# Stick-breaking attention: the sum over later tiles in high and low parts, on TensorE

## The chip, the cores and the metric

One NeuronCore of a Trainium2 chip runs the whole program. The metric is the device time of one execution in microseconds (us); of several executions the median is given. The engines are called by the profile's names: PE is TensorE (PEld its weight loads), DVE is VectorE, ACT is ScalarE, POOL is GpSimd, SP is SyncE.

## What is computed

The program is a stack of layers over 512 tokens of width 1024 in float32: a Mamba layer, a sparse-attention layer, their feed-forward parts, and then a second block with three mixers side by side. The change touches one of these mixers, stick-breaking attention with 8 heads of width 64:

```
z = einsum("bqhd,bkhd->bhqk", q[:, q0:k_len], k[:, :k_len]) * scale
mask = s_idx[None, :] < t_idx[:, None]
log_1m = where(mask, log_sigmoid(-z), 0.0)
after = cumsum(log_1m, axis=3, reverse=True) - log_1m
att = where(mask, exp(log_sigmoid(z) + after), 0.0)
out = einsum("bhqk,bkhd->bqhd", att, v[:, :k_len])
```

With softplus(z) = -log_sigmoid(-z), the exponent is z minus the sum of softplus(z) over the key itself and all later keys before the query. That sum over keys is what the changed lines compute.

## The kernel before, in words

Every engine has its own instruction stream, written out by hand; semaphores join them. The dense products (`product`, L282) take weights and inputs as a high part and a low part in the type fp32r, and make three products of them (high by high, high by low, low by high), each of 512 columns.

The stage of the change is `sb_tensor` (L2047), `sb_scalar` (L2119) and `sb_vector` (L2162). Keys lie on the 128 partitions, queries along the columns. Since only earlier keys count, key tile 0 meets 512 queries, tile 1 meets 384, tile 2 meets 256 and tile 3 meets 128: 1280 columns a head, spread over three PSUM banks (`ZT`, `IN_BANK`, `ZB`; two sets of banks, used by heads in turn).

For head n the steps are:

- PE: the scores z, four f32 products of 64 rows (L2080), and a bf16 product of identity and mask for each diagonal tile (L2085).
- ACT: the absolute value of each bank into `s_e` (L2143), then over all 1280 columns at once the exponential of minus that (L2146) and the logarithm of one plus that (L2148).
- DVE: the softplus, max(z, 0) + `s_e`, bank by bank into `s_sp` (L2180), two buffers in turn. Then three sums of 128 columns of tiles further on (L2186, L2187, L2189) into `sq`, as `later_sums` lays out, so that PE need not add tile by tile.
- PE: subtracts the sums in the same banks. `ntri`, a triangle of minus ones, takes each tile's own part (L2096: four f32 products, of 512, 384, 128 and 256 columns). `nones`, all minus ones, takes the later tiles (L2100: five f32 products over 768 columns in all).
- ACT: the exponential of each bank into `s_e` (L2153).
- PE: the products with the values, for two heads together (L2115, `values_of_pair`); ACT (L2160) and DVE (L2172) split the result in a high and a low part.

On PE the order is: scores of head n, sums of head n-1, the values of a pair when n is odd and at least 3, scores of head n+1. The scores of head n+1 write the banks that head n-1 used, so each bank waits for its exponential at L2153. On ACT the order is: absolute values, exponential and logarithm of head n, and then the exponentials of head n-1. The next stage's products wait for the last `yb_lo` (L2200). The scores of head 7 are followed on PE by the sums of head 6, the values of heads 4 and 5, the sums of head 7, and the values of heads 6 and 7.

Of the kernel before, what the change touches and what calls it, by code (L numbers as in the profile page):

```python
# [6 lines left out]
ALU = mybir.AluOpType  # L7
ACT = mybir.ActivationFunctionType
AX = mybir.AxisListType
F32 = mybir.dt.float32  # L10
# [3 lines left out]
P = 128  # L14
T = 512
# [125 lines left out]
def build(nc, dram):  # L141
    units, at = unit_list()
    NU = len(units)
    with ExitStack() as ctx:
# [3 lines left out]
        def sbuf(name, width, dt=F32, scope=ctx, parts=P):  # L148
            return scope.enter_context(nc.sbuf_tensor(name, [parts, width], dt))
# [1405 lines left out]
        g_row, g_row2, g_cum = g_qs[0], g_qs[1], g_qs[3]  # L1555
        blk = ctx.enter_context(ExitStack())
        s_q, s_k = sbuf("s_q", 4 * T, scope=blk), sbuf("s_k", 4 * T, scope=blk)
        s_sp = [sbuf(f"s_sp{i}", 1280, scope=blk) for i in range(2)]
        s_e = [sbuf("s_e0", 1280, scope=blk)]
        s_identb, s_negb = sbuf("s_identb", P, BF16, scope=blk), sbuf("s_negb", P, BF16, scope=blk)  # L1560
        blk.close()
        blk = ctx.enter_context(ExitStack())
        sbuf("below_yc", 16 * KC * T // 4, scope=blk)
        s_e += [sbuf(f"s_e{i}", 1280, scope=blk) for i in (1, 2, 3)]
        blk.close()
        s_vt = mod_w

# [461 lines left out]

        ZT = [(0, 0, 0, 512), (1, 0, 512, 384), (2, 0, 1024, 256), (1, 384, 896, 128)]  # L2030
        uS = at["sb"]
        later_done = S("later_done")

        def later_sums(m):

            return sq[:, m % 2 * T:m % 2 * T + 2 * P], sq[:, m % 2 * T + 2 * P:m % 2 * T + 3 * P]

        def later_keys(m):

            sp, (of0, of1) = s_sp[m % 2], later_sums(m)  # L2040
            o1, o2, o3 = (ZT[i][2] for i in (1, 2, 3))
            return (((0, 1, sp[:, o1:o1 + P]), (0, 2, of0)), ((1, 1, sp[:, o2:o2 + P]), (1, 2, of1)),
                    ((2, 1, sp[:, o3:o3 + P]),))

        IN_BANK = ((0,), (1, 3), (2,))

        def sb_tensor(pe):  # L2047
            def aux(t):
                pe.wait_ge(bx_done, t + 1)
                if t == 8:  # L2050
                    pe.wait_ge(go_done, 4)
                if t >= 10:
                    pe.wait_ge(bt_done, t - 9)
                for s in range(TT):
                    ins = pe.transpose((B4, B5)[t % 2][:, s * P:(s + 1) * P], sq[:, (t % 2) * T + s * P:(t % 2) * T + (s + 1) * P], ident)
                ins.then_inc(b_aux, 1)

            for t in range(1, 12):
                if t >= 2:
                    pe.wait_ge(bx_done, t - 1)  # L2060
                product(pe, uS + t, h_hi, h_lo)
                if t <= 4:
                    stat_sums(pe, *norms[f"gdn_{t - 1}"], 1)
                if t >= 9:
                    aux(t - 1)
            aux(11)
            pe.wait_ge(bx_done, 12)
            pe.wait_ge(bt_done, 4)
            pe.wait_ge(gnrm, 4)
            pe.wait_ge(smask_done, 2)  # L2070
            for n in range(10):
                if n < 8:
                    t, hs = n // 2, slice(n % 2 * 64, n % 2 * 64 + 64)
                    for b, tiles in enumerate(IN_BANK):
                        if n >= 2:
                            pe.wait_ge(ea_done, 3 * (n - 2) + b + 1)
                        out = ZB[n % 2][b]
                        for i in tiles:
                            _, c, o, w = ZT[i]
                            pe.matmul(out[:, c:c + w], s_k[hs, t * T + i * P:t * T + (i + 1) * P],  # L2080
                                      s_q[hs, t * T + i * P:(t + 1) * T], start=(i != 3), stop=False,
                                      skip_group_check=True)
                        for i in tiles:
                            c = ZT[i][1]
                            ins = pe.matmul(out[:, c:c + P], s_identb[:, :], s_negb[:, :], start=False, stop=False,  # L2085
                                            skip_group_check=True)
                        ins.then_inc(z_mm, 1)
                if 1 <= n < 9:
                    m = n - 1
                    pe.wait_ge(sp_done, m + 1)  # L2090
                    pe.wait_ge(later_done, 3 * m + 3)
                    for b, tiles in enumerate(IN_BANK):
                        out, keys = ZB[m % 2][b], later_keys(m)[b]
                        for i in tiles:
                            _, c, o, w = ZT[i]
                            pe.matmul(out[:, c:c + w], cst("ntri"), s_sp[m % 2][:, o:o + w], start=False,  # L2096
                                      stop=(i == 3), skip_group_check=True)
                        for i, j, src in keys:
                            c = ZT[i][1]
                            ins = pe.matmul(out[:, c + j * P:c + j * P + src.shape[1]], cst("nones"), src, start=False,  # L2100
                                            stop=(i == 2 or j == 2), skip_group_check=True)
                        ins.then_inc(acc_mm, 1)
                if n >= 3 and n % 2:
                    values_of_pair(pe, (n - 3) // 2)
# [57 lines left out]
        def sb_vector(v, link):  # L2162
            v.tensor_copy(s_identb[:, :], ident).then_inc(smask_done, 1)
            v.tensor_scalar(s_negb[:, :], cst("strict"), 1.0, -NEG, ALU.subtract, ALU.mult).then_inc(smask_done, 1)
            for t in range(8, 12):
                v.wait_ge(b_aux, t - 7)
                v.tensor_copy(s_vt[:, :].rearrange("p (s c) -> p s c", s=TT)[:, :, (t - 8) * P:(t - 7) * P],
                              (B4, B5)[t % 2][:, :].rearrange("p (s c) -> p s c", s=TT)).then_inc(bt_done, 1)
# [5 lines left out]

            for n in range(8):
                v.wait_ge(ln_done, n + 1)
                if n >= 2:
                    v.wait_ge(acc_mm, 3 * n - 3)
                for b, (o, w) in enumerate(ZPARTS):
                    ins = v.scalar_tensor_tensor(s_sp[n % 2][:, o:o + w], ZB[n % 2][b][:, 0:w], 0.0,  # L2180
                                                 s_e[n % 4][:, o:o + w], ALU.max, ALU.add)
                ins.then_inc(sp_done, 1)
                sp, (of0, of1) = s_sp[n % 2], later_sums(n)
                o1, o2, o3 = (ZT[i][2] for i in (1, 2, 3))
                v.wait_ge(sp_done, n + 1)
                v.tensor_tensor(of1, sp[:, o2 + P:o2 + 2 * P], sp[:, o3:o3 + P], ALU.add).then_inc(later_done, 1)  # L2186
                v.tensor_tensor(of0[:, 0:P], sp[:, o1 + P:o1 + 2 * P], sp[:, o2:o2 + P], ALU.add).then_inc(later_done, 1)  # L2187
                v.wait_ge(later_done, 3 * n + 2)
                v.tensor_tensor(of0[:, P:2 * P], sp[:, o1 + 2 * P:o1 + 3 * P], of1, ALU.add).then_inc(later_done, 1)  # L2189
                if n >= 4 and n % 2 == 0:  # L2190
                    low((n - 4) // 2)
            low(2)
# [820 lines left out]
```

## Time and profile before

| what | value |
|---|---|
| three runs | 2622.99, 2623.27, 2633.18 us; median 2623.27 |
| the profiled execution | 2631.3 us |
| its span | 2629.5 us |
| PE, DVE, ACT, POOL busy | 97%, 46%, 41%, 37% of the span |

### The profile page before, as it was taken

How to read it: one execution, taken by the hardware profiler on the slowest of the kernel's cores; microseconds unless marked ns; L12 is line 12 of the kernel's file. 1: busy time of each engine (PE TensorE's matmuls, PEld its weight loads, DVE VectorE, ACT ScalarE, POOL GpSimd, SP SyncE). 2: the span in 40 equal slices, each digit the busy share in tenths (PEclk: the TensorE clock that was granted, in tenths of full speed). 3: DMA queues.
4: the chain of work that ended last, by engine and by line, in shares of the span. 5: the costliest groups of instructions: out<-in, count | busy, mean ns of one | idle time of the engine just before them, and what ended most of it. 6: DMA issues, size and time to landing. Idle time of an engine off the chain costs nothing.

```text
span 2629.5 us, 37049 instructions
## 1 busy us (share of the span) xinstructions
PE 2538.4 (97%) x13464; PEld 2065.5 (79%) x13464; DVE 1208.7 (46%) x2023; ACT 1069.2 (41%) x1679; POOL 961.2 (37%) x427
## 2 busy tenths in 40 slices
PE   7999989999999989999999999999999999999998
PEld 5777768877888756669888888788668888988887
DVE  4877776577555746655111127654222112631112
ACT  3366644322225346654222226733442323542232
POOL 0333334455464310013444353302214455353453
PEclk9999999999999999999999999999999999999999
DMA  6533334577653310011333231201113333132331
GB/s 249 181 112 115 104 125 138 175 233 231 217 191 111 120 35 28 19 34 57 111 97 100 92 112 57 81 17 41 57 33 100 106 107 112 64 111 86 99 105 56
DMA packets 76195, 277.35 MB, mean 105 GB/s; under 512 B 8576, under 2 KB 11264, under 8 KB 74528
## 3 DMA queue, kind: packets, MB, share of 16 engines
q1 hardware_dynamic: 57104, 202.71, 23.7%
q10 hardware_dynamic: 18960, 72.82, 8.0%
q8 instruction: 91, 1.49, 0.2%
q14 instruction: 40, 0.33, 0.0%
HBM read 272.55 MB, written 2.16 MB: 104 GB/s over the span
## 4 chain that ended last, share of the span: by engine, by line
PE 79%; DVE 9%; issue 4%; DMA 4%; ACT 3%; ACTq 1%; DVEq 0%
PE G L295 28%; PE STAT_G L295 26%; DMA mod_w<-in_modw 2%; DVE mod_w L334 2%; PE B L308 2%; PE B L295 2%; PE B L602 2%; PE B L2423 1%; PE B L1357 1%; PE STAT_G L308 1%; PE NRM L1394 1%; PE G L308 1%; ACTq L1123 1%; PE G L602 1%; PE STAT_G L1375 1%
## 5 line engine op out<-in xcount | busy, mean ns | idle before, releaser
L280 POOL TENSOR_TENSOR w_lo<-raw,w_hi 128x1024 fp32r<-128x1024 f32 x371 | 922.4, 2497 | 1617.2 <-ACT w_hi L272 1550.9
L272 ACT ACTIVATE w_hi<-raw 128x1024 fp32r<-128x1024 f32 x375 | 386.3, 1051 | 304.0 <-PE STAT_G L295 132.2
L295 PE MATMUL G<-h_hi,w_hi 128*128 128x512 f32 x872 | 346.1, 397 | 0.9 <-DVE tn L1001 0.9
L295 PE MATMUL STAT_G<-h_hi,w_hi 128*128 128x512 f32 x856 | 338.0, 395 | 4.4 <-ACT mod_w L1242 1.5
L295 PE MATMUL G<-h_lo,w_hi 128*128 128x512 f32 x872 | 340.2, 390 | 0.0
L295 PE MATMUL G<-h_hi,w_lo 128*128 128x512 f32 x872 | 340.1, 390 | 0.0
L295 PE MATMUL STAT_G<-h_hi,w_lo 128*128 128x512 f32 x856 | 333.4, 389 | 0.0
L295 PE MATMUL STAT_G<-h_lo,w_hi 128*128 128x512 f32 x856 | 333.1, 389 | 0.0
L334 DVE SCALAR_TENSOR_TENSOR mod_w<-mod_w,const 128x1024 f32<-128x1024 f32 x96 | 189.2, 1990 | 50.0 <-DMA mod_w<-in_modw 49.8
L295 PEld LDWEIGHTS G<-h_hi,w_hi 128*128 128x128 f32 x872 | 164.3, 188 | 40.3 <-issue 7.3
L295 PEld LDWEIGHTS STAT_G<-h_hi,w_hi 128*128 128x128 f32 x856 | 160.7, 188 | 40.2 <-issue 4.7
L295 PEld LDWEIGHTS G<-h_lo,w_hi 128*128 128x128 f32 x872 | 164.3, 188 | 34.3 <-issue 1.4
L295 PEld LDWEIGHTS G<-h_hi,w_lo 128*128 128x128 f32 x872 | 164.0, 188 | 34.5
L295 PEld LDWEIGHTS STAT_G<-h_hi,w_lo 128*128 128x128 f32 x856 | 160.8, 188 | 33.8
L295 PEld LDWEIGHTS STAT_G<-h_lo,w_hi 128*128 128x128 f32 x856 | 160.8, 188 | 33.6 <-issue 1.2
L941 ACT ACTIVATE u_hi<-tn 128x512 f32 (+1 forms) x76 | 48.0, 632 | 256.4 <-DVE tn L1001 220.5
L295 PE MATMUL G<-u_hi,w_hi 128*128 128x512 f32 x376 | 147.0, 391 | 0.3 <-issue 0.3
L295 PE MATMUL G<-u_hi,w_lo 128*128 128x512 f32 x376 | 146.3, 389 | 0.0
L295 PE MATMUL G<-u_lo,w_hi 128*128 128x512 f32 x376 | 146.3, 389 | 0.0
L295 PE MATMUL STAT_G<-u_hi,w_hi 128*128 128x512 f32 (+1 forms) x320 | 125.8, 393 | 3.6 <-ACT y L2574 2.7
L295 PE MATMUL STAT_G<-u_lo,w_hi 128*128 128x512 f32 (+1 forms) x320 | 125.1, 391 | 0.0
L295 PE MATMUL STAT_G<-u_hi,w_lo 128*128 128x512 f32 (+1 forms) x320 | 125.0, 391 | 0.0
(581 smaller groups left out, 4440.4 us busy)
## 6 DMA issues: line engine op xcount, KB each, us to landing
raw<-in_units SPq DMA_DIRECT2D x373, 512.0 KB, 3.6
mod_w<-in_modw ACTq DMA_DIRECT2D x96, 512.0 KB, 4.7
acsb<-acs ACTq DMA_DIRECT2D x16, 512.0 KB, 3.7
mod_first<-in_modw ACTq DMA_DIRECT2D x6, 1024.0 KB, 22.5
cw<-in_cw ACTq DMA_DIRECT2D x2, 2048.0 KB, 9.0
x<-in_x SPq DMA_DIRECT2D x2, 1024.0 KB, 12.3
mod_first<-in_modw SPq DMA_DIRECT2D x2, 1024.0 KB, 25.0
raw<-in_units ACTq DMA_DIRECT2D x2, 512.0 KB, 18.8
```

Of the source, the lines that this page charges most:

```text
L272: act.activation(w_hi[s][:, :], raw[s][:, :], ACT.Identity).then_inc(hi_done, 1)
L280: pool.tensor_tensor(w_lo[s][:, :], raw[s][:, :], w_hi[s][:, :].bitcast(F32), ALU.subtract).then_inc(lo_done, 1)
L295: ins = pe.matmul(out[0:m, :], a[s][:, k * P:k * P + m], b[:, c], start=(n == 0 and q == 0), stop=(n == len(blocks) - 1 and q == 2))
L308: ins = pe.matmul(out[:, tokens[a]], w[s][:, k * P:(k + 1) * P], b[:, at_tokens(k, a)], start=(k == 0 and q == 0), stop=(k == n - 1 and q ...
L334: ins = v.scalar_tensor_tensor(half_row, half_row, 1.0, silc, ALU.mult, ALU.mult, accum_out=mod[:, bass.ds(g * 2 + b, 1)] if not isinstanc ...
L602: ins = pe.matmul(banks[e][0:m[e], tokens[a]], w[s][:, k * P:k * P + m[e]], b[:, at_tokens(k, a)], start=(k == 0 and q == 0), stop=(k == K ...
L941: act.activation(u_hi[g % 2][:, bass.ds(i * (body * T) + j * T, T)], tn[:, (k % 2) * T:(k % 2 + 1) * T], ACT.Identity).then_inc(hh_done, 1)
L1123: act.dma_start(swapped[t % 2][h + a:h + a + 8, :], src[h + b:h + b + 8, :]).then_inc(turn_in[t % 2], 16)
L1357: pe.matmul(out[:, h * T:h * T + w], qr[t % 2][hs, qt * P:w], keys[hs, j * T:j * T + w], start=True, stop=False, skip_group_check=True)
L1375: ins = pe.transpose(TB_[:, o], pr[b % 3][:, o], ident)
L1394: ins = pe.matmul(OB_[hs, qt * P:(qt + 1) * P], vals[:, s * 256 + hd * 64:s * 256 + (hd + 1) * 64], ptr[b % 2][:, h * T + s * P:h * T + (s ...
L2423: ins = pe.matmul(Y[j][64 * hh:64 * hh + 64, s * P:T], xdt[j][:, s * P + 64 * hh:s * P + 64 * hh + 64], seg[:, hh * 1280 + o:hh * 1280 + o ...
```

## The change

`s_sp` and the partial sums in `sq` go. The softplus is written in place over `s_e`. DVE then writes a high part `s_hi` (a copy of all 1280 columns to fp32r) and a low part `s_lo` (`s_e` minus `s_hi`, 1280 columns), one buffer of each. PE multiplies both parts by an fp32r copy of the two constants (`s_minus`, made once by DVE). With no partial sums, PE takes every later tile by itself: the all-ones products are now of 384, 256 and 128 columns for tile 0, 256 and 128 for tile 1, and 128 for tile 2.

```diff
-        s_sp = [sbuf(f"s_sp{i}", 1280, scope=blk) for i in range(2)]
+        s_hi, s_lo = sbuf("s_hi", 1280, F32R, scope=blk), sbuf("s_lo", 1280, F32R, scope=blk)
...
+        s_minus = sbuf("s_minus", 2 * P, F32R, scope=blk)
...
+        LATER_KEYS = (((0, 1, 1), (0, 2, 2), (0, 3, 3)), ((1, 1, 2), (1, 2, 3)), ((2, 1, 3),))
+        KEY_TILE = {1: (512, 384), 2: (1024, 256), 3: (896, 128)}
...
                     pe.wait_ge(sp_done, m + 1)
-                    pe.wait_ge(later_done, 3 * m + 3)
                     for b, tiles in enumerate(IN_BANK):
-                        out, keys = ZB[m % 2][b], later_keys(m)[b]
+                        out = ZB[m % 2][b]
                         for i in tiles:
                             _, c, o, w = ZT[i]
-                            pe.matmul(out[:, c:c + w], cst("ntri"), s_sp[m % 2][:, o:o + w], start=False,
-                                      stop=(i == 3), skip_group_check=True)
-                        for i, j, src in keys:
-                            c = ZT[i][1]
-                            ins = pe.matmul(out[:, c + j * P:c + j * P + src.shape[1]], cst("nones"), src, start=False,
-                                            stop=(i == 2 or j == 2), skip_group_check=True)
+                            for part in (s_hi, s_lo):
+                                pe.matmul(out[:, c:c + w], s_minus[:, 0:P], part[:, o:o + w], start=False,
+                                          stop=(i == 3 and part is s_lo), skip_group_check=True)
+                        for i, j, key in LATER_KEYS[b]:
+                            c, (o, w) = ZT[i][1], KEY_TILE[key]
+                            for part in (s_hi, s_lo):
+                                ins = pe.matmul(out[:, c + j * P:c + j * P + w], s_minus[:, P:2 * P], part[:, o:o + w],
+                                                start=False, stop=(key == 3 and part is s_lo), skip_group_check=True)
                         ins.then_inc(acc_mm, 1)
...
             v.tensor_scalar(s_negb[:, :], cst("strict"), 1.0, -NEG, ALU.subtract, ALU.mult).then_inc(smask_done, 1)
+            a = CONST["ntri"]
+            v.tensor_copy(s_minus[:, :], const[:, a:a + 2 * P]).then_inc(smask_done, 1)
...
                 v.wait_ge(ln_done, n + 1)
-                if n >= 2:
-                    v.wait_ge(acc_mm, 3 * n - 3)
+                e = s_e[n % 4]
                 for b, (o, w) in enumerate(ZPARTS):
-                    ins = v.scalar_tensor_tensor(s_sp[n % 2][:, o:o + w], ZB[n % 2][b][:, 0:w], 0.0,
-                                                 s_e[n % 4][:, o:o + w], ALU.max, ALU.add)
-                ins.then_inc(sp_done, 1)
-                sp, (of0, of1) = s_sp[n % 2], later_sums(n)
-                o1, o2, o3 = (ZT[i][2] for i in (1, 2, 3))
-                v.wait_ge(sp_done, n + 1)
-                v.tensor_tensor(of1, sp[:, o2 + P:o2 + 2 * P], sp[:, o3:o3 + P], ALU.add).then_inc(later_done, 1)
-                v.tensor_tensor(of0[:, 0:P], sp[:, o1 + P:o1 + 2 * P], sp[:, o2:o2 + P], ALU.add).then_inc(later_done, 1)
-                v.wait_ge(later_done, 3 * n + 2)
-                v.tensor_tensor(of0[:, P:2 * P], sp[:, o1 + 2 * P:o1 + 3 * P], of1, ALU.add).then_inc(later_done, 1)
+                    ins = v.scalar_tensor_tensor(e[:, o:o + w], ZB[n % 2][b][:, 0:w], 0.0, e[:, o:o + w],
+                                                 ALU.max, ALU.add)
+                link(ins)
+                if n:
+                    v.wait_ge(acc_mm, 3 * n)
+                v.tensor_copy(s_hi[:, :], e[:, :]).then_inc(sp_hi, 1)
+                v.wait_ge(sp_hi, n + 1)
+                v.tensor_tensor(s_lo[:, :], e[:, :], s_hi[:, :].bitcast(F32), ALU.subtract).then_inc(sp_done, 1)
```

`link` marks an instruction and lets DVE wait until it has ended. `acc_mm` counts the banks whose sums are subtracted, three a head.

## Rows read from the trace of the kernel before

**Rows 1.** The page: an engine's busy share, and the chain's shares by engine.

```profile
PE 2538.4 (97%) x13464; PEld 2065.5 (79%) x13464; DVE 1208.7 (46%) x2023; ACT 1069.2 (41%) x1679; POOL 961.2 (37%) x427
PE 79%; DVE 9%; issue 4%; DMA 4%; ACT 3%; ACTq 1%; DVEq 0%
```

**Rows 2.** Windows: length, each engine's busy time (instructions), granted clock, DMA share, GB/s.

```profile
1876.00:1947.00 71.00, 68.86 (x304) 39.82 (x304) 21.94 (x53) 46.05 (x69) 0.00 (x0) 0.93 0.00 1
...
335.00:340.00 5.00, 4.28 (x17) 1.81 (x18) 3.69 (x6) 3.04 (x4) 3.65 (x2) 0.66 0.03 7
1885.00:1890.00 5.00, 5.00 (x15) 2.94 (x16) 1.49 (x6) 3.96 (x5) 0.00 (x0) 0.62 0.02 3
1890.00:1907.00 17.00, 16.97 (x85) 10.34 (x83) 6.55 (x18) 11.72 (x18) 0.00 (x0) 1.00 0.00 0
```

**Rows 3.** The chain of work through the stage: start, duration, engine, tile, line.

```profile
1886.28 1.81 PE B L2096 x2
...
1891.13 1.05 PE B L2080 x2
...
1893.40 0.22 PE B L2085 x2
...
1894.41 0.91 PE B L2096 x2
...
1897.97 1.12 PE B L2080 x2
...
1901.33 0.91 PE B L2096 x2
...
1904.64 0.22 PE B L2100 x2
1904.86 2.31 PE G L2115 x16
1907.17 1.05 PE B L2080 x2
...
1933.40 0.91 PE B L2096 x2
...
1939.24 1.05 PE B L2096 x2
...
1942.95 0.39 ACT s_e L2153
```

**Rows 4.** The timeline, ACT and DVE in the loop.

```profile
1883.41 1.62 DVE L2180 SCALAR_TENSOR_TENSOR s_sp<-B,s_e 128x512 f32<-128x512 f32 x3 [7.17 <-ACT s_e L2148]
...
1897.34 0.58 ACT L2153 ACTIVATE s_e<-B 128x512 f32<-128x512 f32 x1
...
1904.38 0.69 DVE L2180 SCALAR_TENSOR_TENSOR s_sp<-B,s_e 128x512 f32<-128x512 f32 x1 [4.44 <-ACT s_e L2148]
...
1906.04 0.29 DVE L2186 TENSOR_TENSOR sq<-s_sp 128x128 f32<-128x128 f32 x1
```

**Rows 5.** The chain elsewhere: fp32r products, 256 columns (L602) and 512 (L295).

```profile
452.06 0.71 PE B L602 x6
...
1952.92 5.44 PE G L295 x24
```

**Rows 6.** Groups of DVE by shape: busy, mean ns of one, idle before.

```profile
L2664 DVE TENSOR_SCALAR seg<-acsb,atok 128x512 f32<-128x512 f32 x32 | 15.4, 481 | 0.0
L2664 DVE TENSOR_SCALAR seg<-acsb,atok 128x128 f32<-128x128 f32 x32 | 9.0, 281 | 0.0
L2676 DVE TENSOR_TENSOR seg<-seg,cbm 128x1280 f32<-128x1280 f32 x32 | 46.2, 1487 | 1.4 <-ACT seg L2545 1.4
```

**Rows 7.** The timeline of DVE ahead of the loop.

```profile
1842.52 0.22 DVE L2164 TENSOR_SCALAR s_negb<-const 128x128 bf16<-128x128 f32 x1
1862.81 0.69 DVE L2167 COPY mod_w<-B 128x512 f32<-128x512 f32 x1 [20.06 <-PE B L2055]
```

More of the change, by code:

```diff
@@ L2031, in build @@
         uS = at["sb"]
[L2032 to L2040, printed above, removed]
-            o1, o2, o3 = (ZT[i][2] for i in (1, 2, 3))
-            return (((0, 1, sp[:, o1:o1 + P]), (0, 2, of0)), ((1, 1, sp[:, o2:o2 + P]), (1, 2, of1)),
-                    ((2, 1, sp[:, o3:o3 + P]),))
+        sp_hi = S("sp_hi")
+        LATER_KEYS = (((0, 1, 1), (0, 2, 2), (0, 3, 3)), ((1, 1, 2), (1, 2, 3)), ((2, 1, 3),))
+        KEY_TILE = {1: (512, 384), 2: (1024, 256), 3: (896, 128)}
         IN_BANK = ((0,), (1, 3), (2,))
@@ L2069, in sb_tensor @@
             pe.wait_ge(gnrm, 4)
-            pe.wait_ge(smask_done, 2)
+            pe.wait_ge(smask_done, 3)
             for n in range(10):
@@ L2176, in sb_vector @@
                 v.wait_ge(ln_done, n + 1)
-                if n >= 2:
-                    v.wait_ge(acc_mm, 3 * n - 3)
+                e = s_e[n % 4]
                 for b, (o, w) in enumerate(ZPARTS):
-                    ins = v.scalar_tensor_tensor(s_sp[n % 2][:, o:o + w], ZB[n % 2][b][:, 0:w], 0.0,
-                                                 s_e[n % 4][:, o:o + w], ALU.max, ALU.add)
-                ins.then_inc(sp_done, 1)
-                sp, (of0, of1) = s_sp[n % 2], later_sums(n)
-                o1, o2, o3 = (ZT[i][2] for i in (1, 2, 3))
-                v.wait_ge(sp_done, n + 1)
-                v.tensor_tensor(of1, sp[:, o2 + P:o2 + 2 * P], sp[:, o3:o3 + P], ALU.add).then_inc(later_done, 1)
-                v.tensor_tensor(of0[:, 0:P], sp[:, o1 + P:o1 + 2 * P], sp[:, o2:o2 + P], ALU.add).then_inc(later_done, 1)
-                v.wait_ge(later_done, 3 * n + 2)
-                v.tensor_tensor(of0[:, P:2 * P], sp[:, o1 + 2 * P:o1 + 3 * P], of1, ALU.add).then_inc(later_done, 1)
+                    ins = v.scalar_tensor_tensor(e[:, o:o + w], ZB[n % 2][b][:, 0:w], 0.0, e[:, o:o + w],
[6 more added lines that the diff above has]
+                v.tensor_tensor(s_lo[:, :], e[:, :], s_hi[:, :].bitcast(F32), ALU.subtract).then_inc(sp_done, 1)
                 if n >= 4 and n % 2 == 0:
```

## The prediction

> **What bounds the kernel now.** I read the page first, then the windows, then the chain and the timeline of the stage. PE is busy for 97% of the span and carries 79% of the chain [rows 1], so time saved on PE counts, unless another engine ends last in the stage at hand. The stage with the changed lines lies between 1876 and 1947 us: 71 of 2629.5 us, with POOL idle and a mean granted clock of 0.93 [rows 2]. Whatever the change does must happen in those 71 us, 2.7% of the span. A difference of 0.5%, 13 us, is about what a measurement of this kernel can tell from no change; it would take 18% of the stage.
>
> In the chain the stage looks like PE alone [rows 3]. The timeline shows a second engine close behind. There are two kinds of steps. In a short step PE goes from the scores of head n to the sums of head n-1 and then to the scores of head n+1. The sums of head 1 start at 1894.41 and the scores of head 3 at 1897.97, 3.56 us later [rows 3]. Meanwhile ACT makes absolute value, exponential and logarithm of head 2, and only then, at 1897.34, the first exponential of head 1, which ends at 1897.92 [rows 4] and frees the bank that the scores of head 3 write. **ACT and PE end within 0.05 us of each other.** In a long step, the values of a pair stand between: sums at 1901.33, values at 1904.86, scores at 1907.17 [rows 3], 5.84 us, and there ACT is done long before. The scores take 3.36 us after a short gap (1897.97 to 1901.33), and 3.28 us after a long one, as the loop's period shows: the four sums between heads 1 and 7 that start a pair lie (1933.40 - 1901.33)/2 = 16.04 us apart [rows 3], and 16.04 = 3.56 + 3.36 + 5.84 + 3.28.
>
> **The sums on PE.** Now they take 1904.86 - 1901.33 = 3.53 us a head [rows 3]. The new ones are 20 fp32r products, two each of ten shapes: one of 512 columns, two of 384, three of 256, four of 128. At the higher clock, 2.4 GHz, 24 products of 512 take 5.44 us, 0.227 each, and six of 256 take 0.71, 0.119 each [rows 5]. Between them I take 0.173 for 384. No fp32r product of 128 columns is shown. 
>
> **The work on DVE.** Softplus stays as it is: three instructions, whose start lies 3.05 us after the end of the scores (1904.38 against 1901.33) and whose successor starts 1.66 us later, at 1906.04 [rows 3, 4], that is 4.71 us after the scores. Three small sums go. A copy of 1280 columns comes; the SBUF-only single-source rows give 481 ns for 512 columns and 281 for 128 [rows 6], 0.52 ns a column and 0.21 us fixed: 0.88 us for 1280. If the fp32r output or some other thing keeps it from that pace, it costs like a two-source instruction, 1.49 us. Below, nothing better than 0.88 is shown; I take no gain. The subtraction has two sources and 1280 columns: 1.49 us [rows 6]. With 0.04 us at each handover the low part is ready for PE at 4.71 + 0.88 + 0.04 + 1.49 + 0.04 = 7.16 us after the end of the scores.
>
> The Trainium skill has a rule for the copy (VectorE: DVE Perf Modes, What auto-detection actually checks): a single source with source and destination in SBUF runs at two elements a cycle, a two-source f32 operation at one. The rows' slopes agree, 0.52 ns a column on the one and about 1.2 per column all told on the other [rows 6]; whether fp32r as output is within the rule, no row shows.
>
> **The new wait.** The copy waits for the sums of the head before (`acc_mm`), since there is one buffer. Queued behind it on DVE are the copy, the subtraction and at times the split of a pair's result; PE's next sums wait for them. In a short step these sums end 2.74 us after the scores, before the softplus is done at 4.71, so the wait costs nothing. If that cover went, it would cost what the sums overran. The constant's copy is one DVE instruction ahead of the loop, like the 0.22 us ones there, and 20.06 us of idle time follow [rows 7]: nothing, and uncovered some 0.3 us. DMAs, SP and POOL are not touched; ACT's work is the same.
>
> **Put together.** A short step stays at 3.56 us: PE is done 0.8 us sooner, but ACT's exponential, 3.5 us after the scores, holds the next scores. After these scores, 3.56 + 3.36 = 6.92 us after the last ones, PE wants the low part and gets it at 7.16: a new wait of 0.24 us. The long step then costs 2.74 + 2.31 + 3.28. A pair takes 7.16 + 8.33 = 15.49 us against 16.04, **0.55 less**. There are two such pairs up to the scores of head 6: 1.10 us.
>
> At the start: softplus of head 0 starts at 1883.41 [rows 4] and ends at 1885.07; the low part is ready at 1885.07 + 2.45 = 1887.52, where the sums started at 1886.28 [rows 3]. The clock is at its lower level, 1.2 GHz, until about 1888.8 (granted 0.62 between 1885 and 1890, 1.00 after) [rows 2]. So 1.28 us yield 0.64 of the 2.74, the rest takes 2.10: the next scores start at 1890.90 against 1891.13, a gain of 0.23.
>
> At the end the values of heads 4 and 5 follow the sums of head 6, and then come the sums of head 7, with no scores between as cover. They start 5.84 us after the scores now (1939.24 against 1933.40) [rows 3] and 7.16 after: 1.32 lost, which eats the 0.23 + 1.10 gained. What is left is the last sums: now 1939.24 to the end of the last exponential at 1943.34 [rows 3], 4.10 us. After, the first bank's sums take 1.26 us, the exponentials of two banks follow at 0.60 each or as the sums allow, and the last, of 0.39, ends at 3.30. Gain 0.80. **Sum: 0.23 + 1.10 - 1.32 + 0.80 = 0.8 us faster.** Against the profiled execution's own 2631.3 that is 2630.5; it is 8 us above the median of the runs, with the stage the same, and against the median 2623.27 it is **2622.5**.
>
> **Rivals.**
>
> - **The low part comes later or narrow products are dear.** A copy of 1.49 us costs 0.61 more at four places (the start, the waits for heads 2 and 4, head 7): 2.4 us, giving 2624.9. Narrow products at 0.22 add 0.88 in three places and 0.7 at the end, 3.3 us: 2625.8. Both: 2628.2. For it: no row shows either operation with fp32r.
> - **The narrow products are cheap**, 0.07: 0.32 less at three places and some 0.3 at the end, 2621.2. If, against the timeline, ACT did not hold the short steps, all eight sums would save 0.8 to 1.1 us each, and the time would be 2614 to 2617. Against it: the 0.05 us between ACT's exponential and the scores.
> - **TensorE's clock falls in the loop: slower.** At the start of the loop PE ran at 1.2 GHz for some 10 us after a gap. The change puts new idle gaps into PE's stream: 1.2 us at the start, 1.1 us in each pair, 1.3 at the end. If the clock stayed low for the loop, PE's 14.4 us a pair (3.36 + 3.28 + 2 x 2.74 + 2.31) would become 28.9 and a pair lose 12.8 against now; over three pairs and a half, some 45 us: 2668. It passes 13 us where about 26 us of the stage's full-clock work run at the lower clock. Against it: PE stays 93% busy in the new loop, and low clock appears in short stretches (0.66 over 5 us, with 4.28 busy, is 3.4 us at half) [rows 2], worth 1.7 us each; one or two of these are possible, 2624 to 2626. The Trainium skill (TensorE: Matmul & The Clock Gate, HAM oscillation) says that idle gaps between bursts of products bring the clock to half; it speaks against this change, and its oscillation in every step would be the 2668.
> - **The change does not do what it says**: the products run at f32's pace after all, 5120 columns at twice two records' price, about 8.5 us a head. That is 5 us more in each of eight: 2663. The dense products of the same type at 0.227 [rows 5] speak against it.
>
> **How the numbers follow.** Chances: the forecast with its small terms either way (2621 to 2624) 0.60; dear copy or dear narrow products 0.18; cheap narrow products or free short steps 0.08; a short loss of clock 0.09; clock low through the loop 0.03; f32's pace 0.01; a gain of over 13 us out of this stage, for which I see no term, 0.01. Clock and f32's pace are slower by over 0.5%: 0.04. Faster by over 0.5%: 0.01. The rest is within 0.5%: 0.95. The range starts at 2619.5, under the cheap products by some 1.5 for what an unshown price hides. Upward, both dear terms give 2628 and a stretch of low clock 2630; and one of the three runs of before lies 9.9 above the median, as the profiled one lies 8.0 above, so a median of after may fall there: 2633.
>
> **What would show it.** Right: sums (L2096 and L2100's successors) of 2.7 us a head; the copy at 0.88 and the subtraction at 1.49; in short steps the scores still waiting for ACT's exponential; a wait of DVE's low part of 0.2 us in each pair, and of 1.3 at head 7; pairs 15.5 us apart; one stretch of low clock at the start. Wrong: pairs 16 us or more apart, low clock after 1890, sums over 3.5 us, or short steps of under 3.5 us.

## The result and the profile after

The changed kernel takes 2629.48 us, median of 20 runs (2624.69 to 2637.75), against 2624.56 us for the kernel before (20 runs, 2621.57 to 2633.18). The ratio is 1.0019, with a 95% interval of 1.0011 to 1.0027: **4.9 us slower**, where 0.8 us faster was forecast. The profiled execution took 2634.37 us, its span is 2632.6 us. In the two traces the difference lies in the stage of the change: its loop starts 1.0 us earlier after the change (1875.36 against 1876.35), the next stage starts 3.1 us later, and from there to the end both take 682.3 us. Up to 1850 us the granted clock is 0.99 in both, with PE busy for 1773.95 us before and 1774.36 after. The work ahead of the loop differs by more than the change from one execution to the next: in the 14 profiled executions of this study the loop starts between 1864.6 and 1876.5 us. So a single time says little here; medians, and distances inside the stage, say more.

On the page of the changed kernel PE's busy time is unchanged and DVE's is 13 us longer; the lines answer to [rows 1].

```profile
PE 2537.8 (96%) x13480; PEld 2071.7 (79%) x13480; DVE 1221.4 (46%) x2016; ACT 1069.2 (41%) x1679; POOL 961.6 (37%) x427
PE 79%; DVE 9%; issue 4%; ACT 3%; DMA 3%; ACTq 1%; DVEq 0%
```

Shorter sums should have lowered PE's busy time. That they did not is the first hint: the new products took longer than their price. The windows of the stage show why (columns: length, PE busy and instructions, granted clock, DMA share, GB/s). First the changed kernel, then the kernel before, whose rows list all engines' busy times ahead of the clock:

```profile
1875.00:1892.00 17.00, 15.44 (x45) 0.60 0.00 1
1892.00:1900.00 8.00, 7.22 (x36) 1.00 0.00 1
1900.00:1905.00 5.00, 4.97 (x19) 0.66 0.00 0
1905.00:1917.00 12.00, 11.22 (x64) 1.00 0.00 1
1917.00:1922.00 5.00, 4.88 (x19) 0.66 0.00 0
1922.00:1934.00 12.00, 11.21 (x64) 1.00 0.00 0
1934.00:1939.00 5.00, 4.86 (x19) 0.66 0.01 3
1939.00:1950.00 11.00, 9.01 (x64) 1.00 0.00 0
```

```profile
1875.00:1892.00 17.00, 16.17 (x48) 8.25 (x47) 5.84 (x14) 9.60 (x13) 0.00 (x0) 0.70 0.02 7
1892.00:1909.00 17.00, 16.97 (x80) 10.03 (x80) 4.81 (x12) 11.26 (x17) 0.00 (x0) 1.00 0.00 1
1909.00:1926.00 17.00, 16.97 (x83) 10.05 (x81) 5.41 (x13) 11.57 (x19) 0.00 (x0) 1.00 0.00 0
1926.00:1943.00 17.00, 16.89 (x85) 10.71 (x83) 5.41 (x13) 11.60 (x19) 0.00 (x0) 1.00 0.00 1
```

Before, the clock is at its lower level, 1.2 GHz, only at the loop's start, for 10.2 us ((1 - 0.70)/0.5 x 17). After, it stays there for 13.7 us at the start and falls again **behind each of the three short steps**, for 3.4 us each time ((1 - 0.66)/0.5 x 5). The chain shows what lies under these stretches (start, duration, engine, tile, line; L2073 is the scores, L2089 and L2094 the sums, L2109 the values):

```profile
1891.63 1.05 PE B L2073 x2
...
1897.94 0.49 ACT s_e L2147
1898.43 0.04 issue
1898.48 1.12 PE B L2073 x2
...
1902.04 1.22 PE B L2089 x2
1903.26 1.39 PE B L2094 x6
...
1906.29 2.30 PE G L2109 x16
...
1919.00 1.22 PE B L2089 x2
...
1923.30 2.30 PE STAT_G L2109 x16
```

The sums of head 2 take 1906.29 - 1902.04 = 4.25 us and those of head 4 4.30, against 3.53 us before [rows 3] and 2.74 forecast. The fall comes after the short step's gap, which is new. In the changed kernel's timeline PE waits for ACT before the scores of head 3:

```profile
1897.42 0.28 PE L2094 MATMUL STAT_G<-s_lo,s_minus 128*128 128x128 f32 x1
1897.85 0.58 ACT L2147 ACTIVATE s_e<-B 128x512 f32<-128x512 f32 x1
...
1898.48 1.12 PE L2073 MATMUL B<-s_q,s_k 64*128 64x512 f32 x2 [0.78 <-ACT s_e L2147]
```

What each part costs is best read from where head 2's, 4's and 6's scores start, counted from head 0's, and from the start of the next stage's first product. The table holds these distances in us for every kernel of this study; each row is one profiled execution. Ratio is against the kernel before in the same rounds. Below, head 0 to 2 is called the start, 2 to 4 and 4 to 6 the two pairs, and 6 to end the end.

```
kernel   head 0 to 2   2 to 4   4 to 6   6 to end   stage    ratio [95% interval]
before      14.71      16.04    16.03     24.06     70.84
after       16.20      16.97    17.00     24.73     74.90    1.0019 [1.0011, 1.0027]
e1          15.79      19.83    15.70     24.69     76.01    1.0015 [1.0005, 1.0025]
e2          17.06      16.19    16.18     25.13     74.56    1.0017 [1.0008, 1.0025]
e3          13.92      18.31    15.29     24.10     71.62    1.0010 [1.0001, 1.0019]
e4          14.36      16.03    16.04     24.05     70.48    0.9993 [0.9983, 1.0003]
e5          14.70      15.69    15.69     24.69     70.77    0.9997 [0.9988, 1.0005]
e6          14.67      15.45    15.44     24.70     70.26    0.9997 [0.9988, 1.0006]
e7          14.06      15.39    15.37     23.28     68.10    0.9992 [0.9980, 1.0004]
e8          13.39      15.70    15.70     24.68     69.47    1.0005 [0.9996, 1.0015]
e9          13.82      18.38    15.15     23.94     71.29    1.0003 [0.9993, 1.0013]
e10         13.54      17.89    17.94     22.66     72.03    0.9994 [0.9985, 1.0003]
e11         13.93      14.43    14.43     22.54     65.33    0.9987 [0.9975, 0.9999]
e12         13.20      15.46    15.45     24.68     68.79    0.9990 [0.9981, 0.9999]
```

The change loses 1.5 us up to head 2, 0.9 and 1.0 in the two pairs, 0.7 at the end: 4.06 in the stage, close to the 4.9 of the medians.

### The profile page after: what moved, and what is told of

Same layout as the page of the kernel before. It is cut to its first block, busy times and chain, and to the rows that moved or that the text cites. A ratio compares the mean times of both kernels' runs of the same rounds, so it can differ in the third digit from the quotient of the medians.

```text
span 2632.6 us, 37067 instructions
## 1 busy us (share of the span) xinstructions
PE 2537.8 (96%) x13480; PEld 2071.7 (79%) x13480; DVE 1221.4 (46%) x2016; ACT 1069.2 (41%) x1679; POOL 961.6 (37%) x427
## 3 DMA queue, kind: packets, MB, share of 16 engines
q8 instruction: 91, 1.49, 0.2%
## 4 chain that ended last, share of the span: by engine, by line
PE 79%; DVE 9%; issue 4%; ACT 3%; DMA 3%; ACTq 1%; DVEq 0%
PE G L295 28%; PE STAT_G L295 27%; PE B L308 2%; DMA mod_w<-in_modw 2%; PE B L295 2%; DVE mod_w L334 2%; PE B L602 2%; PE B L2416 1%; PE STAT_G L308 1%; PE G L308 1%; PE NRM L1394 1%; PE B L1357 1%; ACTq L1123 1%; PE G L602 1%; PE STAT_G L602 1%
## 5 line engine op out<-in xcount | busy, mean ns | idle before, releaser
L295 PE MATMUL G<-h_hi,w_hi 128*128 128x512 f32 x872 | 345.7, 396 | 0.5 <-DVE tn L1001 0.5
L295 PE MATMUL STAT_G<-h_hi,w_hi 128*128 128x512 f32 x856 | 338.0, 395 | 4.1 <-ACT mod_w L1242 1.6
L295 PE MATMUL G<-h_lo,w_hi 128*128 128x512 f32 x872 | 340.2, 390 | 0.0
L295 PE MATMUL G<-h_hi,w_lo 128*128 128x512 f32 x872 | 340.2, 390 | 0.0
L295 PE MATMUL STAT_G<-h_hi,w_lo 128*128 128x512 f32 x856 | 333.4, 389 | 0.0
L295 PE MATMUL STAT_G<-h_lo,w_hi 128*128 128x512 f32 x856 | 333.1, 389 | 0.0
L295 PEld LDWEIGHTS G<-h_hi,w_hi 128*128 128x128 f32 x872 | 164.2, 188 | 39.2 <-issue 6.4
L295 PEld LDWEIGHTS STAT_G<-h_hi,w_hi 128*128 128x128 f32 x856 | 160.8, 188 | 39.8 <-issue 4.4
L295 PEld LDWEIGHTS G<-h_hi,w_lo 128*128 128x128 f32 x872 | 164.2, 188 | 34.7
L295 PEld LDWEIGHTS G<-h_lo,w_hi 128*128 128x128 f32 x872 | 164.3, 188 | 34.5 <-issue 1.4
L295 PEld LDWEIGHTS STAT_G<-h_hi,w_lo 128*128 128x128 f32 x856 | 160.6, 188 | 34.0
L295 PEld LDWEIGHTS STAT_G<-h_lo,w_hi 128*128 128x128 f32 x856 | 160.8, 188 | 33.5 <-issue 1.2
L295 PE MATMUL G<-u_hi,w_hi 128*128 128x512 f32 x376 | 147.0, 391 | 0.3 <-issue 0.3
L295 PE MATMUL G<-u_lo,w_hi 128*128 128x512 f32 x376 | 146.3, 389 | 0.0
L295 PE MATMUL G<-u_hi,w_lo 128*128 128x512 f32 x376 | 146.3, 389 | 0.0
L295 PE MATMUL STAT_G<-u_hi,w_hi 128*128 128x512 f32 (+1 forms) x320 | 125.6, 392 | 4.1 <-ACT y L2567 2.7
L295 PE MATMUL STAT_G<-u_hi,w_lo 128*128 128x512 f32 (+1 forms) x320 | 125.1, 391 | 0.0
L295 PE MATMUL STAT_G<-u_lo,w_hi 128*128 128x512 f32 (+1 forms) x320 | 125.0, 391 | 0.0
```

Source lines behind the costliest of these rows:

```text
L295: ins = pe.matmul(out[0:m, :], a[s][:, k * P:k * P + m], b[:, c], start=(n == 0 and q == 0), stop=(n == len(blocks) - 1 and q == 2))
```

## The experiments

The theories: **clock** (the sums' saving opens gaps in PE's stream, TensorE falls to 1.2 GHz, and the next sums run at half speed) against **chain** (the longer DVE work makes PE wait, and the clock is a side show). A third question, whether a fall needs the gap or the new fp32r products, is what e7 and e9 to e11 ask.

Filler in what follows is a dense product of 512 columns into a bank that nobody reads, made of data already in place:

```diff
+        def keep_busy(pe, bank, k):
+            for _ in range(k):
+                pe.matmul(G[bank][:, :], w_hi[0][:, 0:P], h_hi[:, 0:T], start=True, stop=True)
```

### e1: filler in every gap

```diff
             aux(11)
             pe.wait_ge(bx_done, 12)
+            keep_busy(pe, 0, 3)
...
+                    if n == 1:
+                        keep_busy(pe, 0, 2)
+                    if n == 8:
+                        pe.wait_ge(bo_lo, 2)
+                        keep_busy(pe, 1, 4)
...
                         ins.then_inc(acc_mm, 1)
+                if n in (2, 4, 6):
+                    if n == 6:
+                        pe.wait_ge(bo_lo, 1)
+                    keep_busy(pe, 1 if n == 4 else 0, 3)
```

> The changed kernel with products into an unused bank in TensorE's idle gaps (three ahead of the loop, two ahead of the sums of head 0, three after the sums of heads 1, 3 and 5, four ahead of the sums of head 7). Clock theory: the stretches at 1.2 GHz inside the loop (1901.7 to 1904.8, 1918.5 to 1921.9, 1935.8 to 1939 in the changed kernel) go or shrink, and the time comes down from 4.9 us above the kernel before to within 1.5 us of it. Rival, the longer DVE chain alone: filler does nothing for a wait on DVE, so the time stays 4 to 5 us above.

Measured: 2630.02 us, 5.6 above the kernel before's 2624.45. A miss as a whole, and yet the later pair takes 15.70 us where the changed kernel takes 17.00. The clock was kept ahead of the loop, so the first scores and two filler products were done by 1877.9; then PE stood idle for 3.3 us, and the clock was at 1.2 GHz from 1879.8 to 1896.9:

```profile
1881.23 0.80 PE L2099 MATMUL B<-s_hi,s_minus 128*128 128x512 f32 x1 [3.32 <-DVE s_lo L2196]
```

The filler moved the idle time, and a longer fall came behind it.

### e2: the kernel before, its sums late

```diff
                 v.wait_ge(later_done, 3 * n + 2)
+                v.tensor_copy(tn[:, :], sp[:, 0:2 * T])
+                v.tensor_tensor(diag[:, :], sp[:, 0:T], sp[:, T:2 * T], ALU.add)
```

> The kernel before with 1.4 us of idle DVE work ahead of its last small sum, so that PE gets the sums as late as in the changed kernel. DVE chain theory: this alone costs what the change costs, 3 to 5 us. Clock theory: PE's products stay long (f32), the gaps are 0.2 us in short steps, so the waits cost about 2.5 us (1.2 at the start, 1.3 at head 7) and no stretch at 1.2 GHz appears after 1892.

Measured: 2628.46 us, 4.0 above. The pairs lose only 0.15 each and keep the full clock; the windows after the start:

```profile
1872.00:1887.00 15.00, 14.04 (x37) 0.54 0.00 1
1887.00:1944.00 57.00, 54.39 (x262) 1.00 0.00 1
```

The loss of 3.7 us in the stage is at the ends, where nothing covers DVE: 2.35 us up to head 2 and 1.07 after head 6. But not all of it is waiting. Head 0's sums start only 0.5 us later than before (1880.11 - 1869.69 = 10.42 us after the first scores, against 9.93), with this idle time ahead of them:

```profile
1880.11 2.05 PE L2096 MATMUL B<-s_sp,const 128*128 128x512 f32 x2 [0.96 <-DVE sq L2191]
```

Then they take 1886.82 - 1880.11 = 6.71 us for 4.85 before, since the low clock lasts 13.7 us in place of 10.2. So some 1.9 of the 3.7 us is clock again, and 1.9 is the price of late sums alone. The edit also falls a little short of its aim: in the pairs the sums are ready 6.7 us after the scores, not 7.1 as in the changed kernel, so it doesn't make the wait of 0.2 us. The pairs show that lateness of about this size leaves the clock alone there.

### e3: the changed products, a short chain on DVE

```diff
+            v.tensor_scalar(s_lo[:, :], const[:, 0:1280], 0.0, None, ALU.mult).then_inc(smask_done, 1)
...
+                if n:
+                    v.wait_ge(acc_mm, 3 * n)
                 for b, (o, w) in enumerate(ZPARTS):
-                    ins = v.scalar_tensor_tensor(e[:, o:o + w], ZB[n % 2][b][:, 0:w], 0.0, e[:, o:o + w],
+                    ins = v.scalar_tensor_tensor(s_hi[:, o:o + w], ZB[n % 2][b][:, 0:w], 0.0, e[:, o:o + w],
                                                  ALU.max, ALU.add)
-                link(ins)
...
-                v.tensor_copy(s_hi[:, :], e[:, :]).then_inc(sp_hi, 1)
-                v.wait_ge(sp_hi, n + 1)
-                v.tensor_tensor(s_lo[:, :], e[:, :], s_hi[:, :].bitcast(F32), ALU.subtract).then_inc(sp_done, 1)
+                ins.then_inc(sp_done, 1)
```

> The changed kernel's products with a short DVE chain: the softplus is written to the high part directly, the low part is a constant zero (leaves out the low part of the softplus). DVE chain theory: 0.8 to 1.1 us gained in each of four steps and at the end, 4 to 5 us faster than the kernel before. Clock theory: the 0.9 us gaps of the short steps are still there, stretches at 1.2 GHz still follow them, and the time is between 2 us faster and 2 us slower.

Measured: 2626.91 us, 2.5 above, though the short chain no longer delays PE; chain had 4 to 5 us under, and the clock theory's range ended at 2 above. Chain alone falls. The low clock comes behind two of the three short steps:

```profile
1889.00:1897.00 8.00, 8.00 (x33) 0.57 0.00 0
1897.00:1923.00 26.00, 24.45 (x135) 1.00 0.00 1
1923.00:1928.00 5.00, 5.00 (x25) 0.66 0.01 3
```

The pair with the first of them takes 18.31 us, the one without 15.29.

### e4: the kernel before, filler ahead of the loop

The edit is the first hunk of e1 on the kernel before.

> The kernel before with three products into an unused bank in the 0.83 us gap ahead of the loop. Clock theory: the 10 us at 1.2 GHz after 1878.7 shrink or go, 2 to 4 us faster. Rival: that gap has nothing to do with the clock, and the time is the same or 0.5 us slower.

Measured: 2623.60 us, 0.9 under 2624.45, ratio 0.9993, with one inside its interval: unclear, and short of the 2 to 4 us of the clock theory. The low clock shrinks from 10.2 us to 3.4, but the stage only gains 0.36: PE is done with the scores early and waits 2.4 us for ACT and DVE ahead of head 0's sums, and what is left of the low clock now lies on these sums. Low clock costs nothing here where another engine ends last.

### e5: filler in the short steps and ahead of head 0's sums

The changed kernel with the last hunk of e1 and `keep_busy(pe, 0, 3)` at n == 1, nothing else.

> The changed kernel with filler products only in the three short steps' gaps and three ahead of the sums of head 0, none ahead of the loop. Clock theory: no stretch at 1.2 GHz in the pairs, a pair takes 15.7 us (17.0 in the changed kernel, 16.03 before), two pairs give back 2.6 us and the loop's start stays as in the changed kernel, so the time is 1.5 to 3 us above the kernel before. Rival, that filler only moves the clock's fall to another place: 4 to 5 us above.

Measured: 2624.24 us against 2624.78, ratio 0.9997. **The loss is gone.** Pairs of 15.69 us, as expected, and the start comes back too (14.70), which was not; so the time is below the 1.5 to 3 us above that were expected.

```profile
1871.00:1882.00 11.00, 11.00 (x30) 0.53 0.00 0
1882.00:1938.00 56.00, 53.08 (x297) 1.00 0.00 1
```

The stage is 70.77 us, 4.13 less than in the changed kernel, by adding work: 1.50 less up to head 2, 1.28 and 1.31 in the pairs. DVE and ACT do what they did, so this is what the low clock cost. The sums that PE starts after its wait for the low part take 1896.75 - 1893.77 = 2.98 us here, at full clock:

```profile
1893.77 0.73 PE B L2095 x2
...
1896.75 2.31 PE G L2119 x16
```

Every run lists its mean granted clock: the median is 0.985 over the changed kernel's 20 runs, 0.988 over e5's 11 and 0.988 over the 35 of the kernel before in the same rounds. So the fall isn't a matter of the one profiled execution.

### e6: as e5, DVE's chain cut by banks

```diff
                 for b, (o, w) in enumerate(ZPARTS):
-                    ins = v.scalar_tensor_tensor(e[:, o:o + w], ZB[n % 2][b][:, 0:w], 0.0, e[:, o:o + w],
-                                                 ALU.max, ALU.add)
...
+                    link(v.scalar_tensor_tensor(e[:, o:o + w], ZB[n % 2][b][:, 0:w], 0.0, e[:, o:o + w],
+                                                ALU.max, ALU.add))
+                    if n and b == 0:
+                        v.wait_ge(acc_mm, 3 * n)
+                    v.tensor_copy(s_hi[:, o:o + w], e[:, o:o + w]).then_inc(sp_hi, 1)
+                    v.wait_ge(sp_hi, 3 * n + b + 1)
+                    v.tensor_tensor(s_lo[:, o:o + w], e[:, o:o + w], s_hi[:, o:o + w].bitcast(F32),
+                                    ALU.subtract).then_inc(sp_done, 1)
```

PE waits bank by bank for the tiles' own products and takes all later tiles' products after them.

> As the run before, and DVE's chain is cut by banks: softplus, high and low part of a bank are made before the next bank's, and TensorE takes each bank's own product as soon as its parts are there, the later tiles' products after that. Clock and chain theory together: 0.8 us less wait at the start, 0.25 in each pair, 0.8 at head 7, so 1.5 to 2.5 us under the run before, from 1 us above the kernel before to 1 us under it. Clock alone: equal to the run before.

Measured: 2623.43 us against 2624.78, the ratio again 0.9997: 0.8 us under e5 in the medians, not 1.5 to 2.5. Pairs gain the 0.25 us. The start and the end gain nothing: nine smaller instructions with their handovers end 7.87 us after the last scores, not 7.1, which takes back what the earlier first products give.

### e7: f32 sums cut short, in the kernel before

```diff
-            return (((0, 1, sp[:, o1:o1 + P]), (0, 2, of0)), ((1, 1, sp[:, o2:o2 + P]), (1, 2, of1)),
+            return (((0, 1, sp[:, o1:o1 + P]),), ((1, 2, of1),),
```

This leaves out the sum of tile 0 over two column blocks and one of tile 1's.

> The kernel before with f32 sums cut to about 2.9 us a head (leaves out the later-tile products of tile 0 against tile 2 and of tile 1 against tile 2's neighbour, 384 of 768 columns). It has the gap before the scores in short steps, without fp32r and without a longer DVE chain. If the gap that ACT's hold opens is what drops the clock: stretches at 1.2 GHz in some of the pairs, time 0 to 2 us under the kernel before. If narrow fp32r products drop it: 1.00 in all pairs after the start, and 2.5 to 4 us under the kernel before.

Measured: 2620.74 us against 2624.78 (ratio 0.9992, with one inside its interval). The gap is there, and the clock stays:

```profile
1886.63 1.12 PE L2080 MATMUL B<-s_q,s_k 64*128 64x512 f32 x2 [0.68 <-ACT s_e L2153]
```

```profile
1879.00:1934.00 55.00, 50.57 (x241) 1.00 0.00 1
```

This spoke for fp32r's narrow products as the cause. But the gap was 0.68 us, shorter than the changed kernel's 0.78, so it settled nothing; e9 to e11 settle more.

### e8: the changed kernel with filler at the start for full clock

As e5, with e1's three products ahead of the loop and twelve, not three, ahead of head 0's sums.

> The changed kernel with filler ahead of the loop (3), twelve ahead of the sums of head 0 (the 3.3 us idle that the full clock opens there) and three in each short step. Clock theory: clock 1.00 from the loop's start to its end, next scores 1.5 us sooner than in the kernel before, pairs of 15.7 us: 1.5 to 3 us faster than the kernel before. Rival: the start is held by ACT and DVE anyway, and the time is within 1 us of the kernel before.

Measured: 2626.11 us against 2624.78, ratio 1.0005, a miss in the total. The stage did as expected: clock 1.00 throughout, 13.39 us to head 2, the stage 1.37 us shorter than before. Its eleven runs spread over 9 us (2622.44 to 2631.80), and one is inside the interval of the ratio; why the median lies above and not under stays open.

### e9 and e10: longer gaps in the kernel before

```diff
-            return (((0, 1, sp[:, o1:o1 + P]), (0, 2, of0)), ((1, 1, sp[:, o2:o2 + P]), (1, 2, of1)),
-                    ((2, 1, sp[:, o3:o3 + P]),))
+            return (((0, 1, sp[:, o1:o1 + P]),), (),
+                    ((2, 1, sp[:, o3:o3 + P]),))
```

e10 returns ((), (), ()): no later tiles at all. In both, a bank without such a product is counted in `acc_mm` by its last own product.

> The kernel before with f32 sums of 2.65 us a head (leaves out the later-tile products of tile 0 against tile 2 and tile 3 and both of tile 1), so that the idle gap before the scores in a short step is 0.9 us, as in the changed kernel, with f32 products around it. If the gap's length decides: low clock (1.2 GHz) in two or three of the three pairs. If the fp32r products, whose columns fill less of TensorE's time, decide: 1.00 in the pairs, z to z of two heads about 15.2 us.

> As e9, with all later-tile products left out: f32 sums of 2.2 us, gap 1.3 us. Gap's length: low clock in all pairs. fp32r: still 1.00, z to z of two heads about 14.7 us.

Measured: e9 2626.50 us and e10 2622.71 us, against 2624.20; both intervals hold one, so the reading rests on the clock. In e9 PE's gap is 0.91 us (0.78 in the changed kernel; the 0.9 of the expectation was PEld's, 0.92 there), all of the loop's wide products are f32, and the clock falls behind two of three short steps (windows; and the gaps ahead of the two falls):

```profile
1893.00:1901.00 8.00, 8.00 (x24) 0.57 0.00 0
1901.00:1927.00 26.00, 24.19 (x109) 1.00 0.00 1
1927.00:1932.00 5.00, 5.00 (x16) 0.66 0.00 0
```

```profile
1891.84 1.12 PE L2080 MATMUL B<-s_q,s_k 64*128 64x512 f32 x2 [0.91 <-ACT s_e L2153]
...
1925.37 1.12 PE L2080 MATMUL B<-s_q,s_k 64*128 64x512 f32 x2 [0.91 <-ACT s_e L2153]
```

e10 does the same after two of its three gaps of 1.35 us, with 6.8 us at half each time (pairs of 17.89 and 17.94 us), where its expectation had all three. **No fp32r product is needed.** e9 does 0.9 us less PE work a head than the kernel before, 0.2 less than e7, and its pair with the low clock takes 18.38 us. The gap and the work go together in these kernels: a longer gap is also less work for PE, and no run holds the one and changes the other.

### e11: the changed products with no gap

```diff
-                    act.activation(e[:, :], e[:, :], ACT.Exp, scale=-1.0).then_inc(eb_done, 1)
+                    act.activation(e[:, 0:T], e[:, 0:T], ACT.Exp, scale=-1.0).then_inc(eb_done, 1)
                     act.wait_ge(eb_done, n + 1)
-                    act.activation(e[:, :], e[:, :], ACT.Ln, bias=1.0).then_inc(ln_done, 1)
+                    act.activation(e[:, 0:T], e[:, 0:T], ACT.Ln, bias=1.0).then_inc(ln_done, 1)
```

> The changed kernel with ACT's exponential and logarithm over 512 of 1280 columns (leaves out the rest), 1.3 us less on ACT, so that ACT holds no scores: fp32r sums with no gap before the scores and no wait for the low part. If the gap is needed for the clock's fall: 1.00 through the pairs, z to z of two heads 14.4 to 14.6 us, time 4 to 6 us under the kernel before. If fp32r's products are enough by themselves: low clock in the pairs again, 15.5 us or more.

Measured: 2619.41 us against 2624.20, ratio 0.9987 (0.9975 to 0.9999), 4.8 us under. The chain is PE alone, with no gap, and the clock full; sums of 1889.24 - 1886.45 = 2.79 us:

```profile
1886.45 0.52 PE B L2089 x2
...
1889.24 1.05 PE B L2073 x2
```

```profile
1883.00:1930.00 47.00, 46.23 (x263) 1.00 0.00 1
```

Pairs take 14.43 us. The same fp32r products do not drop the clock once ACT has stopped holding the scores. With e5, where filler took the gap's place: no kernel without the gap has a fall after the start, and the fall does not need fp32r. Why some gaps of one length are followed by a fall and others not stays open.

### e12: the best of these

e6 with e1's three products ahead of the loop and eight, not three, ahead of head 0's sums.

> Filler ahead of the loop (3 products), eight ahead of the sums of head 0, three in each short step, and DVE's chain cut by banks. Clock 1.00 through the loop; next scores after head 0 13.3 us from the first ones (14.7 before), pairs of 15.45, end 24.7: the stage 2 to 2.5 us shorter than in the kernel before, the time 1 to 3 us under it, which five rounds may just tell.

Measured: 2622.28 us against 2624.20 over five rounds, ratio 0.9990 (0.9981 to 0.9999): 1.9 us under in the medians, the interval's end just below one, and the stage 2.05 us shorter.

```profile
1868.00:1936.00 68.00, 63.83 (x337) 1.00 0.00 0
```

The median of the runs' mean clock is 0.990, with e4 the highest of the study. It is the only complete version here that is faster than the kernel before beyond its interval, and by very little.

## Why the prediction was wrong

The result lies inside the stated range and within 0.5%, but on the other side of the forecast. Point by point:

- **Prices, right.** The copy takes 0.83 us (0.88 forecast) and the subtraction 1.49, in the changed kernel's groups by shape:

```profile
L2182 DVE TENSOR_TENSOR s_lo<-s_e,s_hi 128x1280 fp32r<-128x1280 f32 x8 | 11.9, 1492 | 0.3
L2180 DVE CAST s_hi<-s_e 128x1280 fp32r<-128x1280 f32 x8 | 6.6, 827 | 2.3 <-PE B L2094 2.1
```

The rule cited from the Trainium skill (VectorE: DVE Perf Modes, What auto-detection actually checks) holds with fp32r as output too: one source, both sides in SBUF, 0.83 us for 1280 columns here and 0.43 for 512 in e6, 0.52 ns a column, as in the f32 rows of [rows 6].

- **Sums at full clock, nearly right, partly by luck.** 2.74 forecast, 2.79 in e11's unbroken stream, but 2.98 in e5 after a wait. A 128-column product is not 0.11: of a pair the second follows after 0.06 and the next product after 0.11, 0.085 on average:

```profile
1896.44 0.22 PE L2089 MATMUL NRM<-s_hi,s_minus 128*128 128x128 f32 x1
...
1896.50 0.27 PE L2089 MATMUL NRM<-s_lo,s_minus 128*128 128x128 f32 x1
...
1896.61 0.33 PE L2094 MATMUL NRM<-s_hi,s_minus 128*128 128x256 f32 x1
```

The 81 ns of the Trainium skill (TensorE: Matmul & The Clock Gate, Back-to-back issue gap) were nearer than my reading of two rows. What these products save, 0.2 us a head, goes into switches of some 0.05 us where a short product comes ahead of a wide one, so two errors cancel; the 2.51 that follows from the 81 ns is further off than 2.74.

- **ACT's hold and the new wait, right.** The changed kernel's next scores start 3.55 us after the last ended (1894.93 to 1898.48), and the sums 7.1 us after (1911.89 to 1919.00; forecast 7.16). The constant's copy and the wait for `acc_mm` cost nothing in the pairs; the copy of head 1 waited 2.08 us for the slow sums of head 0 and was still in time.
- **The start: right until PE starts.** Head 0's sums start 1886.52 - 1875.36 = 11.16 us after the first scores against 9.93 before, 1.23 later as forecast (1.24). I then gave them full clock after 0.64 us of work, because the clock had come back at 1888.8 before. But PE had now stood idle for 1.2 us ahead of these sums, and the clock stayed low until about 1891.3, 13.7 us in place of 10.2: 1891.63 - 1886.52 = 5.11 us of sums for the 3.38 forecast. This is 1.7 us. It was the same mistake as the next one: the wait was priced, and the clock behind it taken over from the trace of before.
- **The step that failed: "Put together".** I let a short step's gap cost nothing, since ACT ends last there anyway, and took 2.74 us for the sums that follow. In the changed kernel the clock falls while the scores behind the gap run, and these sums take 4.25 and 4.30, 1.5 and 1.6 us more, in the two pairs that count (head 6's are covered by DVE's wait ahead of head 7). By e5's 2.98, 1.3 of that is the clock; the other 0.2 is a size, sums that start after a wait. 1.7 + 1.5 + 1.6 = 4.8 us is the difference between the forecast -0.8 and the stage's +4.06. I had the mechanism as a rival, with its price per stretch (1.7 us), and gave it 0.09 for one or two stretches. Two of its signs of being wrong came: pairs of over 16 us, and low clock after 1890. The argument against the rival was a mean: PE 93% busy in the new loop. e7 and e9 show how little a mean says: 50.57 busy of 55 us (92%) with the full clock, and with gaps longer by 0.23 us two falls in three. The rule weighed against the change (Trainium skill, TensorE: Matmul & The Clock Gate, HAM oscillation) says that idle gaps between bursts of products bring the clock to half; it was the one to follow. Its own case is a wait for a DMA in every step of a loop. Here a fall came after seven of nine gaps of 0.78 to 0.91 us, and after none of three of 0.68, and it lasted for part of a step, far from the 2668 us I tied to the rule.
- **The end, nearly right.** Forecast 0.52 us longer from head 6 on (24.58), measured 24.73.
- **With the clock kept in the pairs, the forecast is still 0.7 us too good**: -0.8 us forecast, -0.07 in e5's stage. The two pairs are 0.2 each over the 15.49 forecast (2.98 for 2.74 in the sums), the start 0.22 and the end 0.11. So even without the falls the change gains next to nothing; e6's -0.58 needs another order of work on DVE and PE. That the result lies inside the stated range is owed to margins set for dear products and for the spread of the runs.

## What to carry to other kernels

Work saved on TensorE in a step that another engine ends saves nothing, and the idle time that it opens can cost more than it: where the saving turns into a gap just ahead of the engine's next dense stretch, price the products that follow at the lower clock as well as the higher one, and put the chance of it at even or more unless something fills the gap (9 falls behind the 15 such gaps of the changed kernel, e3, e7, e9 and e10). A busy share over the loop is no argument; list each new gap and what PE did before it. Splitting an operand in two parts also lengthens the chain that feeds the products, and this shows where no other work covers it, in the first and the last turn of the loop.

## What the runs showed of the hardware beyond that

- Three idle gaps of PE of 0.68 us in a short step (e7) were followed by no fall. Gaps of 0.78 to 0.80 us (the changed kernel, e3) and 0.91 us (e9) were followed by one in seven of nine cases, and gaps of 1.35 us (e10) in two of three. The falls did not come in the gap but while the scores behind it ran. This is one trace for each kernel; over all runs the median of the mean clock is 0.985 to 0.987 for these four kernels and 0.988 for e7 and the kernel before.
- A fall inside the loop lasted 3.4 us in the changed kernel and up to 6.8 us in e3, e9 and e10; it cost 1.3 us where 3.4 us of it met the sums (the changed kernel against e5) and 3.2 us where it lasted 6.8 (e9, 18.38 against 15.15). At the start, 6.8 us less of it gained 0.36 (e4).
- Scores made early at full clock can be of no use: e1's left PE 3.3 us idle, and 17.1 us at 1.2 GHz followed; e4's, in the kernel before, left it 2.4 us idle, and 3.4 us followed. Whether the longer idle time or the products behind it make the difference is not shown.
